# Rope of the attention heads read from PSUM by VectorE, squares summed by ScalarE, and the decayed retention product in split form

## What is computed

```python
# layer 0, q and k of each head
q = rope(rms_norm(q.reshape(B, S, A_HEADS, A_HEAD_DIM), q_gain), pos)
k = rope(rms_norm(k.reshape(B, S, A_HEADS, A_HEAD_DIM), k_gain), pos)
# rope: x1, x2 are the halves of a head
jnp.concatenate([x1 * cos - x2 * sin, x2 * cos + x1 * sin], axis=-1)
...
# layer 1, retention: scores with a decay matrix, then the product with v
s = jnp.einsum('bhnqd,bhnkd->bhnqk', qc, kc) * dmat[None, :, None]
inner = jnp.einsum('bhnqk,bhnkd->bhnqd', s, vc)
```

## Time and profile before

| | us |
|---|---|
| median of the runs | 695.58 |
| the profiled execution | 693.75 |
| its span on the core | 692.0 |
| TensorE (matmuls) busy in the span | 665.7 |
| VectorE busy | 415.6 |
| ScalarE busy | 322.9 |
| GpSimd busy | 84.4 |

### The profile page before, as it was taken

How to read it: one execution, slowest core, us unless ns; L and a number is a source line. 1 busy time by engine, 2 the same in 40 slices (tenths; PEclk the granted TensorE clock), 3 DMA queues, 4 the chain that set the end, 5 groups by cost and what they waited for, 6 DMA issues and landing times.

```text
span 692.0 us, 9063 instructions
## 1 busy us (share of the span) xinstructions
PE 665.7 (96%) x3409; PEld 561.8 (81%) x3409; DVE 415.6 (60%) x440; ACT 322.9 (47%) x363; POOL 84.4 (12%) x67
## 2 busy tenths in 40 slices
PE   2997999999999999999999999999999999999997
PEld 2875877788888888889998778778888888888886
DVE  2899855677777545446764445535468777743430
ACT  3844665465555433435334554453355555533320
POOL 3396500000000000002660000000000000000000
PEclk9999999999999999999999999999999999999999
DMA  9964344656655556554755444454646666555600
GB/s 297 328 233 144 101 122 132 218 158 207 184 182 182 198 203 206 184 182 130 235 185 182 137 168 144 161 180 140 198 149 192 193 199 200 187 183 185 210 1 31
DMA packets 81470, 121.95 MB, mean 176 GB/s; under 512 B 2032, under 2 KB 43152, under 8 KB 81440
## 3 DMA queue, kind: packets, MB, share of 16 engines
q1 hardware_dynamic: 80736, 119.55, 53.3%
q0 software_dynamic: 496, 1.90, 0.9%
q10 hardware_dynamic: 208, 0.08, 0.0%
HBM read 120.47 MB, written 1.05 MB: 176 GB/s over the span
## 4 chain that ended last, share of the span: by engine, by line
PE 84%; DVE 8%; ACT 3%; issue 2%; DMA 2%; POOL 1%; SPq 0%; DVEq 0%; ACTq 0%
PE acc L429 18%; PE acc L431 18%; PE acc L430 18%; PE acc L483 17%; PE acc L486 9%; DVE lo L876 3%; ACT hi L671 2%; DMA x<-in_x 2%; POOL small L377 1%; PE scr L499 1%; DVE rot L938 1%; DVE small L924 1%; DVE h_both L885 1%; PE scr L618 1%; PE scr L630 0%
## 5 line engine op out<-in xcount | busy, mean ns | idle before, releaser
L876 DVE TENSOR_TENSOR lo<-raw,hi 128x2048 fp32r<-128x2048 f32 x112 | 259.4, 2318 | 145.5 <-ACT hi L671 144.6
L671 ACT ACTIVATE hi<-raw 128x2048 fp32r<-128x2048 f32 x112 | 214.4, 1916 | 160.2 <-PE acc L431 160.2
L483 PE MATMUL acc<-h_both,hi 128*128 128x512 f32 x512 | 177.8, 394 | 0.0
L486 PE MATMUL acc<-h_both,lo 128*128 128x256 f32 x512 | 141.8, 277 | 0.0
L483 PEld LDWEIGHTS acc<-h_both,hi 128*128 128x128 f32 x512 | 96.0, 188 | 22.2
L429 PE MATMUL acc<-hi,aT_hi 128*128 128x512 f32 x256 | 99.7, 389 | 0.0
L431 PE MATMUL acc<-hi,aT_lo 128*128 128x512 f32 x256 | 99.6, 389 | 0.0
L430 PE MATMUL acc<-lo,aT_hi 128*128 128x512 f32 x256 | 99.6, 389 | 0.0
L486 PEld LDWEIGHTS acc<-h_both,lo 128*128 128x128 f32 x512 | 96.1, 188 | 0.0
L429 PE MATMUL acc<-hi,h_both 128*128 128x512 f32 x224 | 91.3, 407 | 0.0
L431 PE MATMUL acc<-hi,h_both 128*128 128x512 f32 x224 | 87.5, 391 | 0.0
(11 more groups left out here) (116 smaller groups left out, 705.7 us busy)
## 6 DMA issues: line engine op xcount, KB each, us to landing
raw<-in_mlp_w SPq DMA_DIRECT2D x64, 1024.0 KB, 5.4
raw<-in_r_w_in SPq DMA_DIRECT2D x24, 1024.0 KB, 5.1
raw<-in_a_w_qkv SPq DMA_DIRECT2D x12, 1024.0 KB, 5.9
raw<-in_r_w_out SPq DMA_DIRECT2D x8, 1024.0 KB, 5.0
raw<-in_a_w_o SPq DMA_DIRECT2D x4, 1024.0 KB, 5.1
x<-in_x SPq DMA_DIRECT2D x2, 512.0 KB, 11.4
out_x<-x SPq DMA_DIRECT2D x4, 256.0 KB, 4.0
decay_sb<-in_decay POOLq DMA_DIRECT2D x1, 768.0 KB, 5.5
```

Of the source, the lines that this page charges most:

```text
L483: nc.tensor.matmul(bank, feat_view(hi, s)[:, kt, o * P:(o + 1) * P], h_both[:, kt, :, :].rearrange("p b t -> p (b t)"), start=kt == 0, sto ...
L486: m = nc.tensor.matmul(bank[:, 0:SEQ], feat_view(lo, s)[:, kt, o * P:(o + 1) * P], hT_hi[:, kt, :], start=False, stop=kt == KD - 1)
L671: nc.scalar.activation(hi[:, s, :], raw[:, s, :], ACT.Copy).then_inc(hi_ready, 1)
L876: nc.vector.tensor_tensor(lo[:, s, :], raw[:, s, :], hi[:, s, :].bitcast(F32), ALU.subtract).then_inc(lo_ready, 1)
```

## The change

In the attention layer, VectorE multiplies the PSUM bank by sine and cosine itself and adds the two parts (`rope`, now at the place of `raw`). ScalarE then reads the same bank with four squares of 128 columns each, with a sum per row (`head_squares`), in place of a copy and one square of 512 columns; it does so behind the two VectorE products (semaphore `rope_read`). VectorE turns the sums into variances in the new entry `var`, and there releases the bank. GpSimd has only the power left, and for k the product of the tile with its factors. `q_raw` is gone.

In retention, `sT` and v are each split in hi and lo, and the product is formed as `three`, so nine matmuls of fp32r stand in the place of three of fp32. ScalarE writes `v_hi` and `sT_hi`, VectorE `v_lo` and `sT_lo`.

The diff, without declarations of tiles and semaphores:

```diff
--- before.py
+++ after.py
@@ -107,7 +107,7 @@
         for t in range(TT):
             p = 2 * b + t
             at[4 * b + 3 + t].append(("raw", p))
-            at[4 * b + 5 + t].append(("rope", p))
+            at[4 * b + 5 + t].append(("var", p))
@@ -119,7 +119,7 @@
         if O_AT[h] is not None:
             at[O_AT[h]].append(("O", h))
 
-    first_to_last = ["O", "split", "N", "T", "v", "raw", "A", "P", "S", "rope", "E"]
+    first_to_last = ["O", "split", "N", "T", "v", "raw", "var", "A", "P", "S", "E"]
     for k in range(SLOTS):
         at[k].sort(key=lambda what: (first_to_last.index(what[0]), what[1]))
 
...
@@ -381,21 +388,21 @@
 
             norm_power()
             pool.wait_ge(pl.sem, pl.now())
+            pool.sem_inc(tables_g_ready, 1)
             for p_i in range(8):
                 j, t = p_i // 2, p_i % 2
-                raw4 = q_raw[:, p_i % 2, :].rearrange("p (h d) -> p h d", d=P)
-                cos, sin = [rope_g[:, j % 2, t, part, :].unsqueeze(1).broadcast_to([P, 4, P])
-                            for part in range(2)]
-                pool.wait_ge(raw_qk, 2 * p_i + 1)
-                if p_i >= 2:
-                    pool.wait_ge(rotT_ready, p_i - 1)
-                    pool.wait_ge(rot_ready, p_i - 1)
-                nc.gpsimd.tensor_tensor(rot[:, p_i % 2, :].rearrange("p (h d) -> p h d", d=P),
-                                        raw4, cos, ALU.mult).then_inc(u_ready, 1)
-                nc.gpsimd.tensor_tensor(stage_b[:, p_i % 2, :].rearrange("p (h d) -> p h d", d=P),
-                                        raw4, sin, ALU.mult).then_inc(u_ready, 1)
-                power(small[:, 8 + 4 * (p_i % 2):12 + 4 * (p_i % 2)],
-                      small[:, 4 * (p_i % 2):4 * (p_i % 2) + 4], 4)
+                ss = small[:, 4 * t:4 * t + 4]
+                if j % 2 == 0:
+                    at_q = 24 + 8 * t + 4 * (j // 2)
+                    power(small[:, at_q:at_q + 4], ss, 4)
+                else:
+                    pw = small[:, 8 + 4 * t:12 + 4 * t]
+                    power(pw, ss, 4)
+                    r4 = rot[:, t, :].rearrange("p (h d) -> p h d", d=P)
+                    pool.wait_ge(pow_ready, npow)
+                    pool.wait_ge(rot_sum_ready, p_i + 1)
+                    nc.gpsimd.tensor_tensor(r4, r4, pw.unsqueeze(2).broadcast_to([P, 4, P]),
+                                            ALU.mult).then_inc(k_scaled, 1)
 
@@ -517,7 +524,10 @@
 
             def transpose_rot(p_i):
 
-                pe.wait_ge(rot_ready, p_i + 1)
+                if p_i // 2 % 2 == 0:
+                    pe.wait_ge(rot_sum_ready, p_i + 1)
+                else:
+                    pe.wait_ge(k_scaled, 2 * (p_i // 4) + p_i % 2 + 1)
                 if p_i >= 1:
                     pe.wait_ge(qkT_ready, p_i)
                 for h in range(4):
@@ -642,11 +652,13 @@
                 pe.wait_ge(sT_ready, h + 1)
                 pe.wait_ge(v_r_ready, h * 2 + 2)
 
-                nc.tensor.matmul(scr[:, 1, :], sT[:, 0:P], v_r[:, 0, :],
-                                 start=True, stop=True).then_inc(y_ready, 1)
-                nc.tensor.matmul(scr[:, 2, :], sT[:, P:SEQ], v_r[:, 0, :], start=True, stop=False)
-                nc.tensor.matmul(scr[:, 2, :], sT[:, SEQ:384], v_r[:, 1, :],
-                                 start=False, stop=True).then_inc(y_ready, 1)
+                def decayed(dst, columns, t, first_term, last_term):
+                    return three(dst, sT_hi[:, columns], sT_lo[:, columns], v_hi[:, t, :], v_lo[:, t, :],
+                                 first_term, last_term)
+
+                decayed(scr[:, 1, :], slice(0, P), 0, True, True).then_inc(y_ready, 1)
+                decayed(scr[:, 2, :], slice(P, SEQ), 0, True, False)
+                decayed(scr[:, 2, :], slice(SEQ, 384), 1, False, True).then_inc(y_ready, 1)
 
@@ -701,17 +713,19 @@
             norm_squares(0)
             split(0, 2)
 
-            def raw_copy(p_i):
+            def head_squares(p_i):
                 j, t = p_i // 2, p_i % 2
-                if t == 0:
-                    act.wait_ge(tok0_ready, j + 1)
+                act.wait_ge(rope_read, p_i + 1)
+                if p_i == 0:
+                    act.wait_ge(ssq_ready, 4)
                 else:
-                    act.wait_ge(used, 2 * j + 2 + RING)
-                bank = acc[:, p_i % 4, :]
+                    act.wait_ge(squares_qk, 4 * p_i)
                 if p_i >= 2:
-                    act.wait_ge(rot_ready, p_i - 1)
-                nc.scalar.copy(q_raw[:, p_i % 2, :], bank).then_inc(raw_qk, 1)
-                nc.scalar.activation(stage_a[:, p_i % 2, :], bank, ACT.Square).then_inc(raw_qk, 1)
+                    act.wait_ge(pow_ready, p_i)
+                for h in range(4):
+                    nc.scalar.activation(junk[:, h * P:(h + 1) * P], acc[:, p_i % 4, h * P:(h + 1) * P],
+                                         ACT.Square, accum_out=small[:, 4 * t + h:4 * t + h + 1]
+                                         ).then_inc(squares_qk, 1)
@@ -826,8 +840,10 @@
                     if not first:
                         act.wait_ge(y_ready, h * 2)
 
-                    nc.scalar.activation(v_r[:, t, :], acc[:, t, :], ACT.Copy,
-                                         scale=nrm[:, 2, t:t + 1]).then_inc(v_r_ready, 1)
+                    nc.scalar.activation(v_hi[:, t, :], acc[:, t, :], ACT.Copy,
+                                         scale=nrm[:, 2, t:t + 1]).then_inc(v_hi_ready, 1)
+                act.wait_ge(sT_full_ready, h + 1)
+                nc.scalar.activation(sT_hi[:], sT[:], ACT.Copy).then_inc(sT_hi_ready, 1)
                 if not first:
@@ -916,38 +931,43 @@
             norm_factors(0)
             split(0, 2)
 
-            def head_variance(p_i):
-                t = p_i % 2
-                ss = small[:, 4 * (p_i % 2):4 * (p_i % 2) + 4]
-                dve.wait_ge(raw_qk, 2 * p_i + 2)
-                dve.sem_inc(acc_free, 1)
-                own(nc.vector.reduce_sum(ss, stage_a[:, p_i % 2, :].rearrange("p (h d) -> p h d", d=P),
-                                         axis=AX))
-
-                nc.vector.tensor_scalar(ss, ss, nrm[:, 3, t:t + 1], EPS, ALU.mult,
-                                        ALU.add).then_inc(var_ready, 1)
+            own(nc.vector.tensor_scalar(nrm[:, 5, :], nrm[:, 0, :], EPS, None, ALU.mult))
+            own(nc.vector.tensor_scalar(nrm[:, 6, :], nrm[:, 0, :], EPS * P, None, ALU.mult))
+            dve.wait_ge(tables_g_ready, 1)
 
             def rope(p_i):
                 j, t = p_i // 2, p_i % 2
-                u4 = stage_b[:, p_i % 2, :].rearrange("p (h d) -> p h d", d=P)
-                r4 = rot[:, p_i % 2, :].rearrange("p (h d) -> p h d", d=P)
-                pw = small[:, 8 + 4 * (p_i % 2):12 + 4 * (p_i % 2)]
-                dve.wait_ge(u_ready, 2 * p_i + 2)
-                for o in range(2):
-                    a, b = slice(o * 64, o * 64 + 64), slice((1 - o) * 64, (1 - o) * 64 + 64)
-                    dv.mark(nc.vector.tensor_tensor(r4[:, :, a], r4[:, :, a], u4[:, :, b], ALU.add))
-                power_done()
+                raw4 = acc[:, p_i % 4, :].rearrange("p (h d) -> p h d", d=P)
+                cos, sin = [rope_g[:, j % 2, t, part, :].unsqueeze(1).broadcast_to([P, 4, P])
+                            for part in range(2)]
+                u4 = stage_b[:, t, :].rearrange("p (h d) -> p h d", d=P)
+                r4 = rot[:, t, :].rearrange("p (h d) -> p h d", d=P)
+                if t == 0:
+                    dve.wait_ge(tok0_ready, j + 1)
+                else:
+                    dve.wait_ge(used, 2 * j + 2 + RING)
+                if p_i >= 2:
+                    dve.wait_ge(rotT_ready, p_i - 1)
+                sin_done = dv.mark(nc.vector.tensor_tensor(u4, raw4, sin, ALU.mult))
+                nc.vector.tensor_tensor(r4, raw4, cos, ALU.mult).then_inc(rope_read, 1)
+                dve.wait_ge(dv.sem, sin_done)
+                dve.wait_ge(rope_read, p_i + 1)
+                ur = stage_b[:, t, :].rearrange("p (h o d) -> p h o d", o=2, d=64)[:, :, ::-1, :]
+                rr = rot[:, t, :].rearrange("p (h o d) -> p h o d", o=2, d=64)
+                nc.vector.tensor_tensor(rr, rr, ur, ALU.add).then_inc(rot_sum_ready, 1)
+
+            def head_variance(p_i):
+                j, t = p_i // 2, p_i % 2
+                ss = small[:, 4 * t:4 * t + 4]
+                dve.wait_ge(squares_qk, 4 * p_i + 4)
+                dve.sem_inc(acc_free, 1)
                 if j % 2 == 0:
-
-                    heads = slice(24 + 8 * t + 4 * (j // 2), 28 + 8 * t + 4 * (j // 2))
-                    dve.wait_ge(dv.sem, dv.now())
-                    nc.vector.tensor_scalar(small[:, heads], pw, nrm[:, 1, t:t + 1],
-                                            float(P) ** -0.5, ALU.mult,
-                                            ALU.mult).then_inc(rot_ready, 1)
```

(22 more changed lines are left out.)

21 lines of the change are left out of this document (13 added, 8 removed).

## The result

The change makes the kernel slower. Four runs of it have a median of 702.79 us (700.96 to 703.13), four runs of the kernel before beside them 696.04 (695.47 to 696.88): a ratio of 1.0096 with an interval of 1.0076 to 1.0115, or 6.7 us. Another set of runs of the same two kernels gave 700.41 and 695.23, 1.0074 [1.0057, 1.0092], or 5.2 us. The profiled execution of the changed kernel took 702.66 us.

The account below looks back on a forecast made before the run. TensorE, 84% of the chain, was taken to bound the kernel, so only its waits or its own work counted. 693.75 + 7.5 (attention) - 2.1 (retention) = 699.15 us profiled, plus 1.83 to the median: 701.0 us, range 697 to 708.

Parts of the forecast that it names:

- Retention product: Retention's decayed product: nine fp32r matmuls take 2.04 us against 2.57 for three fp32, gaining 2.1 us over four heads.
- The loop of both engines: Attention rope: VectorE's split and products, then ScalarE's squares and `hi`, run in turn, 6.6 to 6.7 us per entry.
- First station: TensorE's scores of head 1 in attention: start at 72.5 us in place of 67.37, 5.1 later.
- Second station: Transposes of head 1's probabilities (L544) in attention: start at 86.2 us in place of 78.26, 8.0 later.
- Third station: Attention's output projection: starts near 113 us in place of 105.25; 7.5 us taken for the whole attention layer.
- The waits at the transposes of the rotated tiles: TensorE at L524 in attention: waits of 1.7 and 1.2 us become smaller ones elsewhere, draining into head 1's wait.
- The clock rival: TensorE's clock falls to 1.2 GHz behind the wait at head 1's scores, adding 2.7 us: 703.7 us; chance 0.22.
- From the profiled execution to the median: Whole kernel: the median of the runs lies 1.83 us above the profiled execution, turning 699.15 into 701.0 us.
- Dear squares: ScalarE's squares in attention take 0.49 us each, the loop 0.84 longer, eight times 6.7 us: 707.7 us; chance 0.15.
- The loop hidden and the stalls gone: Attention: ScalarE and VectorE keep up (loop under 5.8 us per chunk), TensorE's waits go, 6.0 faster: 689.6 us; chance 0.09.

Follow-up runs that it names:

- opened on VectorE: Changed kernel with VectorE taking a slot's rope products ahead of the split in the same slot, ScalarE's order as in the changed kernel: 689.49 us, ratio 0.9914.
- with the wait filled: Changed kernel plus twenty matmuls that nobody reads, run where TensorE waits for head 0's maximum: 700.17 us, ratio 1.0050.
- late squares with the fp32 product: Changed kernel with ScalarE's squares behind the next split's `hi`, and the fp32 retention product of before: 690.77 us, ratio 0.9935.
- the filled kernel before: Kernel before plus thirteen unread matmuls in TensorE's wait of 3.1 us for head 0's maximum: 695.38 us, ratio 0.9986.
- late squares: Changed kernel with ScalarE's four squares of an entry moved behind the next split's `hi`, same instructions: 689.02 us, ratio 0.9905.
- three filled kernels: Unread matmuls in TensorE's wait for head 0's maximum: twenty in the changed kernel (700.17 us), eight in late squares (689.05), thirteen in the kernel before (695.38).
- squares twice: Changed kernel with each head's square computed twice, the first time into columns and a tile nobody reads: 715.71 us, ratio 1.0278.

## Why the prediction was right

It said 701.0 us, 697 to 708, slower; both medians, 702.79 and 700.41, lie in it. Against the runs of before beside them the change costs 6.7 or 5.2 us, where the forecast had 5.4.

- **Retention product, -2.1.** Right: 2.04 us for the nine matmuls, -2.0 us by itself, -2.3 in the stage. What it adds is hidden as the forecast had it. The timeline of VectorE has the last of it far ahead of the second head's product, which starts at 418.75:

```profile
407.25 0.56 DVE L1113 TENSOR_TENSOR sT<-scr,decay_sb 128x384 f32<-128x384 f32 x1 [2.62 <-PE scr L644]
407.72 1.40 DVE L1118 SCALAR_TENSOR_TENSOR v_lo<-acc,nrm,v_hi 128x512 fp32r<-128x512 f32 x2
409.27 0.56 DVE L1124 TENSOR_TENSOR sT_lo<-sT,sT_hi 128x384 fp32r<-128x384 f32 x1
```

- **The loop of both engines.** Right, and shown from three sides: opened on ScalarE, opened on VectorE, and lengthened, with the first station moving by -8.1, -7.8 and +6.4 us. Its terms were 2.20, 1.33, 1.12 and 1.96; they measured 2.20, 1.32, 1.02 and 1.96. The squares took the lower bound, 0.25 us, not the 0.28 that I chose, and the small scaling cost nothing in most turns: 6.5 to 6.64 a turn, not 6.7.
- **First station.** 71.70 against 72.5, by these steps being 0.1 to 0.2 shorter, five times.
- **Second station.** 86.97 against 86.2. Here two errors cancel in part. From the first station the forecast had 13.7 us, and with the wait filled it is 85.38 - 71.71 = 13.67; the changed kernel takes 15.27, and the 1.6 between them is the clock.
- **Third station.** 113.46 against "near 113"; at full clock 111.84. So the term of 7.5 us for the attention layer measured 8.2, but 111.84 - 105.25 = 6.6 without the clock: it was 0.9 too large for what it counted, and the clock, which it left out, made that up. That the sum came so near is luck in this part.
- **The waits at the transposes of the rotated tiles.** The forecast had them "become smaller ones elsewhere (for the bank of entry 0, and for k's product on GpSimd)". The one for the bank did not come: TensorE's chunks go on at 39.4 us with 0.15 idle at most. The one for GpSimd was 3.9 us, larger than the two that went, 2.9. It changed nothing at the station, since all of it drains into the wait of head 1, as the forecast said.
- **The clock rival** is where the argument was wrong. I gave it 0.22, because "the wait of 3.09 us at the scores of head 1 did not bring it". That was one execution. The clock falls in or behind this wait in the second trace of the kernel before and in all other traces in which the wait was left unfilled but one (the late squares with the fp32 product, 2.0 us), and it costs 1.4 to 2.6 us. In the changed kernel it fell in both traces, so what this rival described is what happened; its 703.7 is nearer to the first median, 702.79, and the forecast's 701.0 to the second, 700.41. The slot behind the wait took 76.78 - 72.30 = 4.5 us against 75.21 - 72.28 = 2.9 with the wait filled, 1.6 more, so the price of "2.7 us more" was too high by over half. The Trainium skill, TensorE: Matmul & The Clock Gate, "What's actually happening", has the clock go down after TensorE has idled; eight of the ten unfilled traces agree, and two, with waits of 3.09 and 1.99 us, show no drop. The changed kernel's cost against the kernel before holds little of this, because that kernel loses clock too in most of its runs; the rival counted the loss as wholly new.
- **From the profiled execution to the median, +1.83.** Added as it stood, without a reason. The first trace lacks this clock drop, 1.6 us, and has both MLPs at their shorter length. That most runs lose clock is shown; that 1.83 us is made of it isn't, since the filled kernel before has a median of 695.38 at full clock.
- **Dear squares** fell with 0.25 us each. **The loop hidden and the stalls gone**, 689.6 us, fell as a forecast of this order of instructions: the loop of 6.5 us is over the 5.8 that I set as its point. As a price it was right: with the loop opened the kernel takes 689.0. The rest of its reason holds as well. With GpSimd's rope products gone, VectorE's addition of 512 columns takes 0.69 us in seven of eight cases, where one of 256 took 0.62 on the mean. The eighth runs beside k's product on GpSimd and takes twice as long (timelines of GpSimd and VectorE):

```profile
58.84 1.04 POOL L404 TENSOR_TENSOR rot<-rot,small 128x512 f32<-128x512 f32 x1
...
58.98 1.46 DVE L957 TENSOR_TENSOR rot<-rot,stage_b 128x512 f32<-128x512 f32 x1
```

This is in line with the Trainium skill, SBUF — State Buffer, "SBUF: two separate sides", by which a VectorE instruction with two SBUF inputs and a GpSimd instruction that reads SBUF lock each other out.

## What to carry to other kernels

Where two in-order engines hand work to each other in both directions, follow one item all the way round; if its steps add up to more than the pace of the engine that sets the end, the change can lose although it saves busy time, and moving the waiting instruction behind the independent one can turn the loss into a gain (here from +6.7 to -6.6 us with the same instructions). Compare stations of the trace (the start of a named instruction) as well as whole times, and take more than one trace of the kernel before: a single one lacked a clock drop that nearly all the others have. A term of 2 us is settled by the stage it stands in, when executions of the same kernel differ by as much elsewhere.

## What the runs showed of the hardware that I had not expected

**The clock after short waits.** TensorE's granted clock falls to 1.2 GHz in or behind the wait for head 0's maximum in eight traces, with waits from 2.0 us (late squares) to 7.0 us (squares twice), and costs 1.4 to 2.6 us in the six that have a like trace at full clock beside them. In two traces it doesn't fall (the first trace of before at 3.09 us; late squares with the fp32 product at 2.0 us). Each of the three filled kernels had it at 1.00 at that place. The changed kernel has one more drop, around the wait of 3.9 us for GpSimd, with the fill and without it (0.72 and 0.79 from 56 to 62 us); the first station doesn't show it, since TensorE waits there anyway. What decides between executions stays open.

**The first MLP matrix has two lengths.** Its 256 recorded matmuls of 512 columns start over 88.48 us or over 90.18 us, in either MLP, and nothing lies between. In the first trace of the kernel before (timeline of TensorE, first and last of the first MLP):

```profile
135.31 0.47 PE L483 MATMUL acc<-h_both,hi 128*128 128x512 f32 x1
...
223.79 0.40 PE L483 MATMUL acc<-h_both,hi 128*128 128x512 f32 x1
```

and in its second:

```profile
136.95 0.48 PE L483 MATMUL acc<-h_both,hi 128*128 128x512 f32 x1
...
227.13 0.40 PE L483 MATMUL acc<-h_both,hi 128*128 128x512 f32 x1
```

Same kernel, same granted clock of 1.00, 1.70 us apart. The difference grows evenly from the first matmul to the last: the mean step from one of these matmuls to the next is 0.3470 us in the short length and 0.3537 in the long one. The first trace of before had the short length twice, that of the changed kernel the long one twice, its repetition the short one twice; so the +1.7 and the +1.3 in the accounting of the spans come from this, as it fell. (The +1.3 is 1.7 from this, less 0.4 behind the last matmul; all traces with the split product have this 0.4, and why was not looked at.) The 13 traces hold 18 short and 8 long ones, with no kernel tied to either. What sets it stays open; it was not tried.
